# One of two 16-row vector-matrix products moved from TensorE to GpSimd, and the rows of the other spread over VectorE's steps, in a transformer block on one core

## The reference, cut to what matters

```python
mod_l = split((silu(c) @ w_ada + b_ada)[:, None, :], 6)   # six vectors of 2048; w_ada is 2048 x 12288
n_lat = modulate(rmsnorm(h_lat, g_norm1), mod_l[0], mod_l[1])
mix_lat = mixer_block(n_lat, n_ctx, ...)    # z = n @ w_in: parts u (S5), v (LRU), g, two gates
h_lat = h_lat + mod_l[2] * mix_lat
f_lat = modulate(rmsnorm(h_lat, g_norm2), mod_l[3], mod_l[4])
h_lat = h_lat + mod_l[5] * peer_ffn(f_lat, ...)
```

## Time and profile before

| | us |
|---|---|
| median of 3 runs | 2304.81 (2303.97 to 2306.12) |
| the profiled execution, its own time | 2299.99 |
| its span, first to last instruction | 2298.2 |
| PE busy | 1990.5 (87% of the span) |
| DVE busy | 1370.3 (60%) |
| POOL busy | 1056.3 (46%) |
| ACT busy | 467.8 (20%) |

### The profile page before, as it was taken

One profiled execution on the slowest core, in us unless ns is written; L12 is line 12 of the kernel. 1 busy time (PEld: TensorE's weight loads), 2 busy tenths in 40 slices (PEclk: granted clock), 3 DMA queues, 4 the chain that ended last, 5 costly groups with the idle time before them and its releaser, 6 DMA issues.

```text
span 2298.2 us, 21873 instructions
## 1 busy us (share of the span) xinstructions
PE 1990.5 (87%) x8106; PEld 1152.7 (50%) x8106; DVE 1370.3 (60%) x2154; ACT 467.8 (20%) x1015; POOL 1056.3 (46%) x927
## 2 busy tenths in 40 slices
PE   6999999999999999889998998877777777777777
PEld 4443348888888887764543544422222223222222
DVE  5645964788873544865555456556556665665644
ACT  3116740344441000111101110110111111111011
POOL 0012323898991100355545445555555555545542
PEclk9999999999999999989999999999999999999999
DMA  9967885445558989899999999999999999999996
GB/s 343 331 226 201 311 308 169 135 144 147 146 151 305 378 309 333 312 400 406 417 417 414 417 421 421 422 422 422 421 421 422 422 422 421 422 422 421 421 421 273
DMA packets 253978, 789.34 MB, mean 343 GB/s; under 512 B 25608, under 2 KB 171216, under 8 KB 178480
## 3 DMA queue, kind: packets, MB, share of 16 engines
q0 software_dynamic: 83792, 574.96, 61.5%
q1 hardware_dynamic: 158400, 203.53, 26.8%
q10 hardware_dynamic: 11680, 9.44, 1.3%
HBM read 774.20 MB, written 9.47 MB: 341 GB/s over the span
## 4 chain that ended last, share of the span: by engine, by line
PE 52%; DMA 38%; issue 3%; POOL 3%; DVE 3%; ACT 1%; ACTq 0%; DVEq 0%; SPq 0%; POOLq 0%
DMA vb<-in_peer_v,eidx 34%; PE ps L1338 15%; PE ps L2327 12%; PE ps L2263 4%; PE ps L2207 4%; PE ps L1545 3%; PE ps L1308 3%; PE ps L1323 2%; DMA nT<-in_peer_u,eidx 2%; PE ps L1283 1%; PE ps L1492 1%; POOL vb L1745 1%; PE ps L1574 1%; PE ps L1264 1%; PE ps L1479 1%
## 5 line engine op out<-in xcount | busy, mean ns | idle before, releaser
L2327 PE MATMUL ps<-vb,diag 128*128 128x512 f32 x2048 | 943.6, 608 | 243.6 <-DMA vb<-in_peer_v,eidx 240.7
L2327 PEld LDWEIGHTS ps<-vb,diag 128*128 128x128 f32 x2048 | 376.9, 192 | 797.4 <-DMA vb<-in_peer_v,eidx 398.7
L1745 POOL DMA_INDIRECT vb<-in_peer_v,eidx x256 | 409.0, 1598 | 524.0 <-PE ps L2327 507.4
L2133 DVE CUSTOM_DVE_ANT_0 nT<-nT,f 128x2048 f32<-128x2048 f32 x167 | 382.0, 2291 | 321.0 <-DMA nT<-in_peer_u,eidx 320.6
L1338 PE MATMUL ps<-nT,w_ring 128*128 128x256 f32 (+1 forms) x1472 | 381.6, 417 | 0.0
L1338 PEld LDWEIGHTS ps<-nT,w_ring 128*128 128x128 f32 x1472 | 276.2, 190 | 95.6 <-issue 65.9
L2133 DVE CUSTOM_DVE_ANT_0 mT<-mT,f 128x2048 f32<-128x2048 f32 x84 | 192.2, 2291 | 159.0 <-DMA mT<-in_peer_u,eidx 158.8
L1745 POOL DMA_INDIRECT nT<-in_peer_u,eidx x167 | 187.7, 1124 | 65.6 <-issue 50.0
L1904 ACT ACTIVATE gel<-hd 128x2 f32<-128x2 f32 (+1 forms) x130 | 26.1, 202 | 900.3 <-DVE hd L2133 900.3
L2263 PE MATMUL ps<-fT,w_ring 128*128 128x256 f32 x448 | 103.1, 390 | 9.4 <-issue 8.6
L1884 ACT ACTIVATE diag<-ident,wgt 128x128 f32<-128x128 f32 x256 | 90.8, 394 | 94.3 <-PE ps L2327 80.1
(11 more groups left out here) (410 smaller groups left out, 2160.7 us busy)
## 6 DMA issues: line engine op xcount, KB each, us to landing
w_ring<-in_w_ada SPq DMA_DIRECT2D x80, 1024.0 KB, 8.6
w_ring<-in_w_in SPq DMA_DIRECT2D x50, 1024.0 KB, 7.6
w_ring<-in_w_ada POOLq DMA_DIRECT2D x16, 1024.0 KB, 5.7
w_ring<-in_peer_w_query SPq DMA_DIRECT2D x16, 1024.0 KB, 24.6
w_ring<-in_w_proj_b SPq DMA_DIRECT2D x8, 1024.0 KB, 8.1
w_ring<-in_w_proj_a SPq DMA_DIRECT2D x8, 1024.0 KB, 8.8
w_ring<-in_w_out SPq DMA_DIRECT2D x8, 1024.0 KB, 7.4
vb<-in_w_out SPq DMA_DIRECT2D x5, 1024.0 KB, 13.0
```

What stands on the lines that cost most here:

```text
L1745: pool.indirect_dma_start(row, None, table, bass.IndirectOffsetOnAxis(ap=eidx[:, i % 3, j:j + 1], axis=0))\
L2133: v.tensor_tensor_reduce(u_buffer(m), u_buffer(m), f[:, i // HEADS], 1.0, 0.0, ALU.mult, ALU.add, hd[:, i % 2, m % K:m % K + 1]).then_inc( ...
L2327: last = pe.matmul(ps[:, 4 * tile + c, :], diag[:, m % NDIAG], vb[m % NV][:, c * 512:(c + 1) * 512], start=(r == 0), stop=(r == HEADS * K ...
```

## The change

Three things change, all in `mixer`:

1. Chunk 2 is no longer multiplied on PE. POOL issues its 16 rows into slot 3, each in two halves of 1024 columns (`load_late`), multiplies a half by the coefficients and adds it to a running sum (`sum_late`: one tensor_scalar and, from row 1 on, one tensor_tensor for each half). After row 15 PE sums the two sums over the partitions (`last_rows(0)`, four matmuls), between the third and the fourth pair of g blocks.
2. DVE's 16 rows of chunk 3 are placed otherwise: rows 0 and 1 ahead of `conv(0)`, rows 2 to 5 behind `conv(0)` to `conv(3)`, one in each recurrence step (6 to 13), and rows 14 and 15 in the first two turns of the loop over the g blocks. POOL issues `load_row(n + 1)` behind `sum_late(n)`.
3. Pairs of `w_in` blocks keep to slots 0 to 2 up to the last g pair, where before the last three g pairs already used all five. `late_rows(0)`, DVE's addition of the bias for chunk 2, moves from ahead of the g loop to its turn 6.

```diff
-LATE_PER_PAIR = {3: (1, 0), 4: (3, 1), 5: (3, 1), 6: (3, 1), 7: (2, 1)}
+EARLY_SUMS = 6
...
+            def load_late(n, x):
+                if n == 0:
+                    pool.wait_ge(late_free[0], late_free[1])
+                _, lo, hi = late_sums[x]
+                at = LATE_CHUNKS[0] * D
+                pool.dma_start(row_view(w_ring[:, 3])[:, lo:hi], t["w_ada"][0, n * P:(n + 1) * P, at + lo:at + hi])\
+                    .then_inc(late_in[x], 16)
+
+            def sum_late(n):
+                for x, (total, lo, hi) in enumerate(late_sums):
+                    pool.wait_ge(late_in[x], late_base[x] + 16 * (n + 1))
+                    w = row_view(w_ring[:, 3])[:, lo:hi]
+                    if n == 0:
+                        ins = pool.tensor_scalar(total, w, scol[:, n, 0:1], None, ALU.mult)
+                    else:
+                        link(pool.tensor_scalar(w, w, scol[:, n, 0:1], None, ALU.mult))
+                        ins = pool.tensor_tensor(total, total, w, ALU.add)
+                    if (n, x) == (KD - 1, len(late_sums) - 1):
+                        ins.then_inc(late_done, 1)
+                    else:
+                        link(ins)
+                    if n + 1 < KD:
+                        load_late(n + 1, x)
+
             load_row(0)
+            for x in range(2):
+                load_late(0, x)
...
+            for n in range(EARLY_SUMS):
+                sum_late(n)
+                load_row(n + 1)
             pool.wait_ge(acc_free, V0 + NB)
...
-            load_row(1)
             for k in range(KW):
-                if 2 * k + 2 < KD:
-                    load_row(2 * k + 2)
                 pool.wait_ge(acc_free, U0 + k + 1)
...
-                if 2 * k + 3 < KD:
-                    load_row(2 * k + 3)
+                sum_late(EARLY_SUMS + k)
+                load_row(EARLY_SUMS + k + 1)
+            load_row(EARLY_SUMS + KW + 1)
+            for n in range(EARLY_SUMS + KW, KD):
+                sum_late(n)
             pool.wait_ge(u_out, 128 * KW)
...
+            for k in range(EARLY_SUMS - 4):
+                row_vector(k)
             for k in range(4):
                 conv(k)
-            row_vector(0)
+                row_vector(EARLY_SUMS - 4 + k)
             for k in range(KW):
                 q_of(k)
-                row_vector(2 * k + 1)
+                row_vector(EARLY_SUMS + k)
                 scans(k)
-                if k < KW - 1:
-                    row_vector(2 * k + 2)
...
-            late_rows(0)
...
+                if k < KD - KW - EARLY_SUMS:
+                    row_vector(EARLY_SUMS + KW + k)
                 if k in (2, 3):
                     input_weights(k - 2)
+                if k == KW - 2:
+                    late_rows(0)
...
             for c in range(1, KW // 2):
                 for _ in columns(G0 + 2 * c, T, 2 * T):
                     pass
+                if c == KW // 2 - 2:
+                    last_rows(0)
```

More of the change, by code:

```diff
@@ L112, in build @@
         n_pairs, n_ada = [0], [0]
-        def plan_ada(chunk, k, slot):
-            n_ada[0] += 1
-            return plan(t["w_ada"][0, k * P:(k + 1) * P, chunk * D:(chunk + 1) * D], slot, (ada_used, n_ada[0]))
         def first_half(w, c, slot):
@@ L146, in plan_second @@
             pair_at[n][1] = second_half(w_in, pairs[n], slot, acc_full, 2 * n + 2)
-        n_late = [0]
-        def plan_late(count):
-            for _ in range(count):
-                ada_at.append(plan_ada(*late[n_late[0]], 3))
-                n_late[0] += 1
-        row_free = freed_by[4]
-        freed_by[4] = (last_used, KD)
-        plan_first(NB // 2, turn[NB % 3])
-        plan_second(NB // 2, turn[(NB + 1) % 3])
-        for n, (before, after) in LATE_PER_PAIR.items():
-            plan_first(n + 1, turn[(2 * n + 2) % 3])
-            plan_late(before)
-            plan_second(n + 1, turn[(2 * n + 3) % 3])
-            plan_late(after)
-        last_wide = n + 1
-        n_slot = [turn[(2 * last_wide + 2) % 3]]
+        n_late = [KD]
+        row_free, late_free = freed_by[4], freed_by[3]
+        freed_by[3] = (last_sum, 1)
+        freed_by[4] = (last_used, KD)
+        first_stage = len(pairs) - NSTAGE
+        for n in range(NB // 2, first_stage):
+            plan_first(n, turn[2 * n % 3])
+            plan_second(n, turn[(2 * n + 1) % 3])
+        n_slot = [turn[2 * first_stage % 3]]
         def next_slot():
@@ L176, in plan_last @@
                                 (last_used, len(last_at) + 1)))
-        for n in range(last_wide + 1, len(pairs)):
+        for n in range(first_stage, len(pairs)):
             plan_first(n, next_slot())
@@ L321, in mixer @@
         pwq = sb("pwq", [P, 2, G, Q])
-        kzero = sb("kzero", [H, G, H])
+        kz_all = sb("kzero", [P, G * H])
+        kzero = kz_all[0:H].rearrange("p (g h) -> p g h", g=G)
+        late_b = sb("late_b", [P, D - G * H])
         Cc = sb("Cc", [P, 2, G, H])
@@ L369, in mixer @@
         sums = [(last_c[:, :], 0, 704), (big[:, 13312:14656], 704, 2048)]
+        late_sums = [(kz_all, 0, G * H), (late_b, G * H, D)]
         fin_sum = big[:, 8192:8192 + D]
@@ L1256, in _ @@
             ada_n = [0]
-            def ada_unit(bank):
-                k = ada_n[0] % KD
-                w = row_view(unit(pe, ada_at[ada_n[0]]))
-                ada_n[0] += 1
-                for j in range(4):
-                    last = pe.matmul(ps[32 * j:32 * j + 32, bank, :], scol[:, k, :], w[:, j * 512:(j + 1) * 512],
-                                     start=(k == 0), stop=(k == KD - 1))
-                last.then_inc(ada_used, 1)
-            def late_unit():
-                if ada_n[0] == NFIRST * KD:
-                    pe.wait_ge(acc_free, V0 + 5)
-                ada_unit(6)
             def group_unit(g, x):
@@ L1328, in columns_by_halves, with columns @@
                             last.then_inc(acc_full, 1)
-                        for _ in range(late_at.count((n, j))):
-                            late_unit()
-            def columns(a, lo, hi, spots=((), ())):
+            def columns(a, lo, hi):
                 w = [unit(pe, u) for u in pair_at[a // 2]]
@@ L1343, in columns @@
                             last.then_inc(acc_full, 1)
-                        for _ in range(spots[j].count(k)):
-                            late_unit()
                     yield
             def last_rows(q):
-                pe.wait_ge(last_used, KD * q)
+                if q == 0:
+                    pe.wait_ge(late_done, 1)
+                else:
+                    pe.wait_ge(last_used, KD * q)
                 if q == 2:
@@ L1354, in last_rows @@
                     at = slice(j * 512, (j + 1) * 512)
-                    for total, lo, hi in (sums if q == 1 else [(fin_sum, 0, D)]):
+                    for total, lo, hi in (late_sums, sums, [(fin_sum, 0, D)])[q]:
                         a, b = max(lo, at.start), min(hi, at.stop)
                         if a < b:
-                            last = pe.matmul(ps[32 * j:32 * j + 32, (7, 0)[q - 1], a - at.start:b - at.start],
+                            last = pe.matmul(ps[32 * j:32 * j + 32, (6, 7, 0)[q], a - at.start:b - at.start],
                                              notfirst[:, 1:33], total[:, a - lo:b - lo], start=True, stop=True)
@@ L1442, in _ @@
                 if c == KW - 1:
-                    columns_by_halves(V0 + 2 * c, 0, 2 * T, [(n, j) for n in range(2) for j in range(2)])
+                    columns_by_halves(V0 + 2 * c, 0, 2 * T)
                     break
-                spots = ((), ()) if c < KW // 2 else ((7, 15), (7, 15))
-                for j, _ in enumerate(columns(V0 + 2 * c, 0, 2 * T, spots)):
+                for j, _ in enumerate(columns(V0 + 2 * c, 0, 2 * T)):
                     i = 2 * c + j
@@ L1484, in s5_states @@
                 pe.wait_ge(pt_done, s + 1)
-                pe.wait_ge(u_in, 16 * 4)
+                pe.wait_ge(u_in, 16 * (KD + 4))
                 if s >= 1:
@@ L2147, in _ @@
             tokens(1)
-            v.wait_ge(late_sum, 3)
+            v.wait_ge(late_sum, 4)
             v.wait_ge(mods_out, 112)
```

33 lines of the change are left out of this document (16 added, 17 removed).

## The result

The changed kernel takes 2398.80 us (median of four, 2396.0 to 2400.11) where the kernel before takes 2304.39: a ratio of 1.0408, 95% interval 1.0396 to 1.0420. That is 94 us slower. The prediction had the sign, but said 2331 with a range up to 2350.

A forecast was written before the change was run, and what follows sets the result against it. PE was taken to set the time of this stage. The terms 30.4 - 16.1 + 2 + 2 + 7.2 + 1.2 = 26.7 us, added to the median 2304.8, gave 2331, with an 8 in 10 range of 2311 to 2350.

The forecast's parts named there:

- (a): PE's u blocks without chunk 2's 16 rows: a gain of 16.1 us at most.
- (b): Price of one chunk 2 row on POOL: 9.4 us alone, 13.0 beside DVE, 11.2 taken.
- (c): Early part: convolutions wait for POOL's loads of DVE's rows, so PE's first u block starts 30.4 us later.
- (d): PE's clock drops after two idles, ahead of its first two gates: +2 us (0 to 4).
- (e): Steps of the u blocks: PE needs 16.0 us, POOL 15.4; no loss unless a POOL row costs above 12.
- P: Price in us of one row of chunk 2 on POOL, taken as 11.2, between 9.4 and 13.0.
- (g): PE waits 7.2 us for POOL at last_rows(0); lag_zero at 417.3; what follows 0 to +2, nothing taken.
- (f): Slots for the g pairs: the second half of a pair is loaded later, +2 us for the third pair.
- beyond the sum: Rival, 9%: three loads queue where one did, POOL and DVE await each other's rows; +50 to +60 us, 2355 to 2365.
- POOL's total: Rival, 10%: POOL's own chain, not the convolutions, sets the stage; PE waits 28 us at one place, +15 remain, 2320.

The follow-up runs named there:

- e5: Changed kernel, but VectorE makes chunk 2's sums behind its own rows and POOL only issues the loads: 2322.97 us.
- e6: Changed kernel with POOL's multiplication as tensor_tensor, the coefficient broadcast along the row: 2392.88 us.
- e1: Changed kernel with VectorE's four first convolutions ahead of all its early rows: 2403.3 us.
- e2: Changed kernel with POOL's load of VectorE's next row issued ahead of POOL's sum, not behind it: 2359.01 us.
- e3: Changed kernel without POOL's multiplication (tensor_scalar) in rows 1 to 15: 2354.73 us.
- e10: e5 with POOL making four multiplications and four additions of 512 in each u step, on its own buffer, waited for by nobody: 2338.12 us.
- e4: Kernel before, chunk 2 still on PE, with only VectorE's rows and their loads placed as in the changed kernel: 2328.75 us.
- e9: Kernel before, with twelve of chunk 2's rows moved to VectorE where it idles, four kept on TensorE, none on POOL: 2311.07 us, ratio 1.0035.
- e12: Changed kernel with POOL's first tables made ahead of store_mods(0) and the bias: 2393.23 us, ratio 1.0392 to the kernel before.
- e11: e9 with four slots for the g pairs, last_rows(0) behind the last g pair, and VectorE's step 7 row behind the scan: 2320.90 us, ratio 1.0075.
- e13: Kernel before, ten of chunk 2's rows moved to VectorE, six on TensorE; four g slots, POOL's tables ahead of store_mods(0): 2311.64 us, ratio 1.0034.

## Why the prediction was wrong, by its own steps

**(a)** held: a u step without chunk 2 and without waits is 15.85 us (14.00 + 1.99, less what they overlap), as e5 shows, where PE waits nowhere in the u blocks.

**(b)** was too low: 9.4 to 13.0 with 11.2 taken, and a row took 13.1 even with DVE half idle, where the low end was meant to hold. The additions took 2.3 to 2.9 us, at or under their 2.5 to 3.2; the multiplications lie far outside theirs (2.85 at the least, for 1.1 to 2.2). The nearest row with one input was a memset, and a memset reads nothing. e6 shows that the form makes the difference: with the coefficient as a broadcast tensor the same product takes 1.9.

**(c)** had the right mechanism and was mis-sized: +42.3 for +30.4. POOL issued row 4's load at 207.98 (predicted 201.1), and `conv(3)` was done at 224.79: landing and DVE's two took 16.8, predicted 13.4. PE's `gates(1)` at the lower clock added 1.6. But e1 shows that it was not even the term that counts: with the convolutions out of POOL's reach, the whole is no shorter.

**(d)** held in kind: each idle is followed by a `gates` of 3.6 to 3.8 us instead of 1.99, and then by little more. It happens five times, not twice, after idles of 4.2 to 20.4 us; the five are 8.6 us longer together, where +2 was in the sum, though in the last three the ring sets the pace and not PE.

**(e)** is the step that failed. It says "Nothing, unless P is above 12", from each engine's load by itself: PE 16.0, POOL 15.4, DVE lighter than before. P was above 12, but the lag did not go to (g) alone. `lag_zero` came 61 us behind the forecast 417.3. Of these, 12 are (c) and 3 are (g); but 25 lie between the first u block and the first g block (151.6 us where the sum had 126.5), and 16.8 are PE's wait for the last copy of `zu` inside the first g pair: 42 us at the steps that (e) put at nothing. (The other 4 are longer blocks behind PE's waits in the g columns.) The loads are not what counts; the ring is. e2 breaks it and takes 40 us away, e3 shortens it and takes 44 away, with POOL idle 4.9 to 9.6 us a step. And behind the ring lies a second thing, which I had priced in (c), where DVE's two take 8 us for 6, and left without a price here: POOL's operations hold up DVE's. e2 leaves DVE busy 97 of 100 us, and e10, where nothing waits for POOL, still loses 26 us over the steps. I took DVE's due dates (`conv(4)` two blocks later) from one engine's timeline and never walked from DVE's row through the scans, `q_of`, ACT's roots and the `zu` copy back to POOL.

**(f)** held: 1.62 for 2. But e4, e5 and e9 show how near it was to more: the g pairs have fewer slots while rows still use 3 and 4, and where PE came sooner, that wait was 4 to 12 us.

**(g)** said 7.2, and it was 10.27. "0 to +2, nothing taken" for what hangs on it was wrong: POOL's tables started at 479.09, 7 us ahead of PE's first stage block, where the lead had been 30, and POOL has 18.2 to 20 us of work in a stage where PE has 18.2. e12 takes 8.5 us of the shift at the end of the stages away, 6.6 of them PE's waits for tables, and 5.6 of the time. Another 3.0 is the block behind the stages, 30.87 us at a lower granted clock for 27.89 before (29.58 in e12); why its clock is lower stays open. PE's idle ahead of it is not enough of an answer: 3.26 us here, and in e11 3.66 ahead of the same block at 27.89.

Of the rivals, "beyond the sum" came nearest, and its "POOL and DVE each wait for the other's row" is a part of the ring; but it had 9% and ended at 2365, 34 us short, and its sum was one of prices and not of waits. POOL's total was not the bound (e3). (In that rival, eight times 15.4 from 240.5 is 363.7, not 363.9, which changes nothing.) The whole, in the order of the runs: POOL's arithmetic 76 us (e5), by the ring and by holding up DVE, which the runs do not separate cleanly since they overlap (40 to 44 for either repair); and the spread and the slots, 24 in e5 and 28.6 by itself in e4, each beside one execution of the kernel before. Beside its median they are 18.6 and 24.4, and only so do the parts add up to the 94. No version that I tried beats the kernel before; the two nearest, e9 and e13, are 0.35 and 0.34% slower.

## What to carry to other kernels

Before a step is called free because each engine's load is under the step's time, walk once round every cycle of waits that passes through the edited queue, each queue's order included (here: copy, store, sum, load, row, scan, roots, and the next copy behind the roots), and compare its length with the number of steps that it spans. Where an engine issues loads for another, arithmetic put into its queue is a delay of those loads, and to move the load ahead of it, which costs nothing, was worth about as much here (40 us) as to take half of the arithmetic out (44). And price a VectorE that is near full by what GpSimd's operations take from it, not by GpSimd's own time: an engine with idle time is no room if its work stops a full one.

## What the runs showed of the hardware

A multiplication of 128 x 1024 by a per-partition scalar took GpSimd 2.85 us at the least, more than an addition of two tensors of that size (2.33 at the least) and than the same product with the scalar broadcast as a tensor (1.9).

Where VectorE's scan met GpSimd's addition, it was not slowed in proportion but held until the addition was over. The scan at 329.40 took 3.26 us instead of 1.22; POOL's addition beside it ran from 329.19 for 2.40 us, unstretched, and the scan ended 1.07 behind it. The Trainium skill (SBUF — State Buffer, SBUF: two separate sides) says that of a VectorE operation with two SBUF inputs and a GpSimd operation that reads SBUF, the one that starts first has the shared ports for its whole length, and the other is blocked. This trace agrees for this addition. For POOL's tensor_scalar it agrees only in part: the operation at 325.63, met at 326.25 by one of 2.85, took 2.29 instead of 0.69. So VectorE's was the one held, though it had started first, and only for 1.6 of the 2.85; the two behind it took 0.69 each, as alone, while POOL was still at work. The operations at 302.68 (2.85 for 1.22) and 349.18 (2.18 for 0.69) were met in the same way and lost 1.6 and 1.5. Why it is not the whole length stays open.
